# A two-block transformer kernel on one Trainium2 core: the first pair's products moved into the last gz block, attention's reciprocal and scaling moved ahead of the delta rule's side work, the sink column copied by ScalarE

## The reference, cut to what matters

```python
proj = h @ w_in[l]                      # -> gq, gk, gv, gz, ga, gb, sq, sk, sv
o_g = gated_delta_rule_chunked(q_g, k_g, v_g, g, beta)    # 8 heads of 64, chunks of 64
o_g = rms_norm(o_g, gdn_norm_w[l]) * silu(heads(gz))
# inside the delta rule, per head and chunk:
A  = where(strict, einsum('cd,sd->cs', kb, k) * decay, 0)
qk = where(causal, einsum('cd,sd->cs', q, k) * decay, 0)
# sliding window attention, window 128, 8 query heads on 2 key heads:
s = einsum(q, k) * D ** -0.5 - slopes * dist              # alibi and mask
m = maximum(max(s), sink)
p = exp(s - m);  p = p / (sum(p) + exp(sink - m));  o = p @ v
mixed = concatenate([o_g, o_s]) @ w_out[l]
```

## Time and profile before

| | us |
|---|---|
| median of 3 runs | 1262.69 (1262.55 to 1263.47) |
| the profiled execution | 1261.78 |
| its span | 1259.9 |
| TensorE busy | 1217.9 |
| VectorE busy | 706.5 |
| ScalarE busy | 496.3 |
| POOL busy | 107.1 |

### The profile page before, as it was taken

One profiled execution on the slowest core, in us unless ns is written; L12 is line 12 of the kernel. 1 busy time (PEld: TensorE's weight loads), 2 busy tenths in 40 slices (PEclk: granted clock), 3 DMA queues, 4 the chain that ended last, 5 costly groups with the idle time before them and its releaser, 6 DMA issues.

```text
span 1259.9 us, 20097 instructions
## 1 busy us (share of the span) xinstructions
PE 1217.9 (97%) x8477; PEld 998.4 (79%) x8477; DVE 706.5 (56%) x1031; ACT 496.3 (39%) x780; POOL 107.1 (9%) x151
## 2 busy tenths in 40 slices
PE   3899999999999999999999999999999999999998
PEld 3577788788878888888888889798877678888886
DVE  4699878655467453333323457858566555333344
ACT  4543543565246322212222344223465663232232
POOL 4000003621020000000000110000012310000000
PEclk9899999999999999999999999999999999999999
DMA  9665621002123534233322343333222125333311
GB/s 313 211 222 177 218 79 36 3 3 71 35 67 101 167 102 141 75 117 101 100 88 64 88 144 97 101 84 60 78 68 54 27 64 133 101 88 92 114 38 67
DMA packets 150953, 125.60 MB, mean 100 GB/s; under 512 B 16984, under 2 KB 134513, under 8 KB 150736
## 3 DMA queue, kind: packets, MB, share of 16 engines
q1 hardware_dynamic: 147888, 119.88, 31.6%
q10 hardware_dynamic: 1744, 2.36, 0.5%
q0 software_dynamic: 1232, 2.07, 0.5%
HBM read 122.20 MB, written 2.10 MB: 99 GB/s over the span
## 4 chain that ended last, share of the span: by engine, by line
PE 91%; DVE 3%; ACT 2%; DMA 2%; issue 1%; POOL 0%; ACTq 0%; DVEq 0%; POOLq 0%
PE bank L588 56%; PE bank L681 5%; PE bank L830 5%; PE bank L1293 4%; PE bank L1263 4%; PE bank L1327 3%; PE bank L1182 2%; DMA arena<-in_meta_tokens_dram 1%; PE bank L1014 1%; PE bank L1218 1%; PE bank L1235 1%; PE bank L1195 1%; PE bank L802 1%; PE bank L639 1%; PE bank L789 1%
## 5 line engine op out<-in xcount | busy, mean ns | idle before, releaser
L588 PE MATMUL bank<-hsplit,whi 128*128 128x512 f32 (+1 forms) x1872 | 552.0, 379 | 0.8 <-DVE wlo L2051 0.7
L588 PEld LDWEIGHTS bank<-hsplit,whi 128*128 128x128 f32 x1872 | 341.1, 188 | 73.0 <-issue 8.0
L588 PE MATMUL bank<-hsplit,wlo 128*128 128x512 f32 (+1 forms) x936 | 352.3, 376 | 0.0
L2051 DVE TENSOR_TENSOR wlo<-ring,whi 128x2048 fp32r<-128x2048 f32 (+4 forms) x100 | 200.4, 2005 | 180.0 <-ACT whi L1524 179.7
L1524 ACT ACTIVATE whi<-ring 128x2048 fp32r<-128x2048 f32 (+4 forms) x100 | 168.5, 1685 | 133.2 <-DVE xT L2411 53.3
L588 PEld LDWEIGHTS bank<-hsplit,wlo 128*128 128x128 f32 x936 | 175.9, 188 | 33.1
L588 PE MATMUL bank<-a_split,whi 128*128 128x512 f32 x340 | 104.7, 389 | 0.0
L588 PEld LDWEIGHTS bank<-a_split,whi 128*128 128x128 f32 x340 | 63.8, 188 | 13.2
L588 PE MATMUL bank<-a_split,wlo 128*128 128x512 f32 x170 | 66.1, 389 | 0.0
L2080 DVE SCALAR_TENSOR_TENSOR post<-ring,small,post 128x512 f32<-128x512 f32 x77 | 57.9, 752 | 3.2 <-DMA ring<-in_w_ada_dram 0.5
L1465 POOL TENSOR_TENSOR acc<-acc,tb 128x512 f32<-128x512 f32 x12 | 17.7, 1477 | 424.1 <-ACT tb L1763 424.1
(11 more groups left out here) (456 smaller groups left out, 1731.9 us busy)
## 6 DMA issues: line engine op xcount, KB each, us to landing
ring<-in_w_ada_dram SPq DMA_DIRECT2D x24, 1024.0 KB, 5.4
ring<-in_w_in_dram SPq DMA_DIRECT2D x22, 1024.0 KB, 5.3
ring<-in_w_in_dram SPq DMA_DIRECT2D x34, 512.0 KB, 4.7
ring<-in_w_gate_dram SPq DMA_DIRECT2D x11, 1024.0 KB, 5.3
ring<-in_w_up_dram SPq DMA_DIRECT2D x11, 1024.0 KB, 5.4
ring<-in_w_down_dram SPq DMA_DIRECT2D x8, 768.0 KB, 5.0
ring<-in_w_down_dram SPq DMA_DIRECT2D x8, 640.0 KB, 4.6
ring<-in_w_out_dram SPq DMA_DIRECT2D x4, 1024.0 KB, 5.4
```

What stands on the lines that cost most here:

```text
L588: last = mm(o[0:m, 0:n], w[:, k, c0:c0 + m], rhs(s, k), start=k + i == 0, stop=k == kn - 1 and i == 2)
L2051: split_lo = splitter(dve, None, lambda lo, src, hi: tt(lo, src, hi, ALU.subtract))
```

## The change

`chunk_products(0)` (kk and kq of pair 0) and `chunk_turns(0)` (kt and vt) go into the last gz tile, after its steps 3 and 5; pairs 1 to 3 stay where they were. `gate_rows` of pairs 1, 2 and 3 move one or two steps earlier. VectorE takes the reciprocals of units 0, 1 and 2 before `sides_out(2)`, `sides_out(3)` and the last step instead of inside `window`. POOL's `window(j)` stands before the pair's three products instead of behind them. The copy of the sink column goes from VectorE to ScalarE, between vs and kdup.

```diff
--- before.py
+++ after.py
@@ -751,9 +751,41 @@
                     last = mm(query_tile[:, c:c + 2], hsq[(9 + m) % 2][:, b * P:(b + 1) * P], cst("two"), start=True, stop=True)
                 last.then_inc(*(fill("sqsum") if m == 3 else signal("sqsum_step", m)))
 
+            both_heads = (slice(0, HD), slice(HD, P))
+
+            def product(o, left, right, chunks=range(NC), width=CH, start=True, stop=True):
+
+                for i, n in enumerate(chunks):
+                    for r in both_heads:
+                        last = mm(o[r, i * width:(i + 1) * width], left[r, n, :], right(n)[r], start=start, stop=stop)
+                return last
+
+            def tile_product(name, j, left, right):
+
+                o = open_tile(pe, name, j)
+                product(o, left, lambda n: right[:, n, :]).then_inc(*fill(name, j))
+
+            eye = cst("eye")
+
+            def turned(name, j, left):
+
+                o = open_tile(pe, name, j)
+                product(o, left, lambda n: eye).then_inc(*fill(name, j))
+
+            q_of, k_of, v_of = ([by_chunk(qkv[:, 4 * s + j, :]) for j in range(NJ)] for s in range(3))
+
+            def chunk_products(j):
+                pe.wait_ge(*done("silu", 8 + j))
+                tile_product("kk", j, k_of[j], k_of[j])
+                tile_product("kq", j, k_of[j], q_of[j])
+
+            def chunk_turns(j):
+                turned("kt", j, k_of[j])
+                turned("vt", j, v_of[j])
+
             amid_sq = [{}, {3: [(query_lengths, 0)]}, {3: [(query_lengths, 1)]}, {1: [(query_lengths, 2)], 4: [(ada, 8)]}]
             amid_gz = [{1: [(ada, 9)], 3: [(query_lengths, 3)], 5: [(gate_cols,)], 7: [(gate_rows, 0)]},
-                       {3: [(gate_rows, 1)]}, {1: [(gate_rows, 2)], 7: [(gate_rows, 3)]}, {}]
+                       {1: [(gate_rows, 1)]}, {0: [(gate_rows, 2)], 6: [(gate_rows, 3)]}, {3: [(chunk_products, 0)], 5: [(chunk_turns, 0)]}]
             for m in range(4):
                 project(("sq", m), f"sq{m // 2}", P * (m % 2), P, hx, T, release=m % 2 == 1, between=amid_sq[m])
             for m in range(4):
@@ -821,15 +853,6 @@
                 if 0 <= u - 5 < len(SWU) and SWU[u - 5][1] == 3:
                     let_go("so", SWU[u - 5][0])
 
-            both_heads = (slice(0, HD), slice(HD, P))
-
-            def product(o, left, right, chunks=range(NC), width=CH, start=True, stop=True):
-
-                for i, n in enumerate(chunks):
-                    for r in both_heads:
-                        last = mm(o[r, i * width:(i + 1) * width], left[r, n, :], right(n)[r], start=start, stop=stop)
-                return last
-
             all_quarters = ((0, 0), (1, 1), (0, 1), (1, 0))
 
             def heads_to_chunks(name, j, left, right):
@@ -854,27 +877,11 @@
 
             product_order = [(i, b) for i in range(2) for b in range(NB)]
 
-            def tile_product(name, j, left, right):
-
-                o = open_tile(pe, name, j)
-                product(o, left, lambda n: right[:, n, :]).then_inc(*fill(name, j))
-
-            eye = cst("eye")
-
-            def turned(name, j, left):
-
-                o = open_tile(pe, name, j)
-                product(o, left, lambda n: eye).then_inc(*fill(name, j))
-
-            q_of, k_of, v_of = ([by_chunk(qkv[:, 4 * s + j, :]) for j in range(NJ)] for s in range(3))
-
             for j in range(NJ + 1):
                 if j < NJ:
-                    pe.wait_ge(*done("silu", 8 + j))
-                    tile_product("kk", j, k_of[j], k_of[j])
-                    tile_product("kq", j, k_of[j], q_of[j])
-                    turned("kt", j, k_of[j])
-                    turned("vt", j, v_of[j])
+                    if j:
+                        chunk_products(j)
+                        chunk_turns(j)
                 if j:
                     pe.wait_ge(*copied("kk", j - 1))
                     turned("tA", j - 1, gE[j - 1])
@@ -1424,6 +1431,7 @@
             chunked = lambda name: cst(name).unsqueeze(1).broadcast_to([P, NC, CH])
             times = lambda out, a, b, op=ALU.mult: nc.gpsimd.tensor_tensor(out, a, b, op)
             for j in range(NJ + 1):
+                window(j)
                 if j < NJ:
                     pool.wait_ge(*copied("rows", j, 2))
                     pool.wait_ge(*filled("kq", j))
@@ -1438,7 +1446,6 @@
                         pool.wait_ge(*filled("rows", 3, 2))
                     pool.wait_ge(*done("dT", j))
                     times(inv[j], chunked("eye"), gW[j], ALU.subtract).then_inc(*signal("p0", j))
-                window(j)
             pool.wait_ge(*filled("vs"))
             pool.wait_ge(*filled("ada", 9))
             for j in range(NJ):
@@ -1695,6 +1702,9 @@
                 act.wait_ge(*filled(name, j))
                 A(dst, by_chunk(bank(name, j)[:, :]), ACT.Copy).then_inc(*(passed or read(name, j)))
 
+            act.wait_ge(*arrived("gate", 3))
+            act.wait_ge(*filled("gz", 3))
+            A(sc[:, :, SINK], sinks, ACT.Copy).then_inc(*signal("sinkcol"))
             act.wait_ge(*done("dve_vectors", "skn"))
             for g in range(2):
                 for p in range(2):
@@ -2260,8 +2270,8 @@
             def window(u):
                 if u == 0:
                     dve.wait_ge(*arrived("alibi"))
-                    link(v.tensor_copy(sc[:, :, SINK], sinks))
-                if 0 <= u - 2 < len(SWU):
+                    dve.wait_ge(*done("sinkcol"))
+                if u > NJ and 0 <= u - 2 < len(SWU):
                     sw_sum(u - 2)
                 if u < len(SWU):
                     sw_bias(u)
@@ -2324,6 +2334,8 @@
                     decay_arg(j + 1)
                 decay_mul(j)
             for j in range(NJ + 1):
+                if j >= 2:
+                    sw_sum(j - 2)
                 if j < NJ:
                     sides_out(j)
                 if j:
```

## The result

| | before | after |
|---|---|---|
| median of 21 runs, us | 1262.55 (1261.16 to 1264.40) | 1264.71 (1262.30 to 1266.99) |
| after / before | | 1.0017, 95% interval 1.0011 to 1.0023 |
| the profiled execution, us | 1261.78 | 1264.37 |
| its span, us | 1259.9 | 1262.4 |

The change makes the kernel 2.2 us slower (1.4 to 2.9 by the interval): clear of the noise, but within the 0.2% called "no change". The forecast of 1264.0 us is 0.7 us too low; the range held.

What follows compares the result with a forecast made beforehand. TensorE was taken to bound the kernel, busy 1217.9 of 1259.9 us. A new gap of 3.4 plus clock 1.5, less the old gap 2.1 and its clock 1.5, gave +1.3 us: 1264.0 us, range 1262.3 to 1266.0.

Steps and rivals of the forecast that it cites:

- gap before the first scores: TensorE would wait for ScalarE's key copies before the first scores, near 207 to 210 us: 3.4 us.
- low clock behind it: After the new gap TensorE's clock would run low, costing 1.5 us, bounded between 0 and 3.4.
- old gap: TensorE's 2.1 us wait for POOL's scaling of the second unit, near 226 us, would disappear.
- its clock: The low TensorE clock behind the wait for POOL's scaling, 1.5 us, would disappear with that wait.
- The cover moved away: The first pair's 3.88 us of TensorE work would no longer hide ScalarE's key copies, which end 3.88 us later.
- Rival 1: From 210 us on TensorE's clock stays low longer or falls again: 3.4 us lost, 1265.9 us; chance 0.17.
- Rival 3: The wait for the key copies comes but the clock holds: 1262.9 us; chance 0.09.
- Moved in front of the block's last steps they cost PE the same: The first pair's products and turns, 3.88 us, would take TensorE no longer inside the last gz block.
- So the gap goes in any case, mostly because PE is late itself: Even without gain from reordering, the second unit's scaled tile, at 229.2, would precede TensorE, at 229.4 us.
- VectorE "2.75 us later" and "PE 4.9": VectorE's windows start 2.75 us later, TensorE runs 4.9 us late, so waits for PSUM banks don't bind.
- The sink column on ScalarE: ScalarE's new sink copy, ahead of the key copies, would delay them by 0.1 us, at most 0.21.
- Rival 2: POOL stretches small VectorE operations and a scaled tile comes late: TensorE loses 0.2 to 0.7 us, 1264.6 us; chance 0.08.

Runs made afterwards that it cites:

- e2: Changed kernel without the reordering and with the sink copy back on VectorE, leaving the move and the gate rows; 1265.69 us, ratio 1.0022 to the kernel before.
- e8: Changed kernel with only the first pair's products in the gz block, its turns kept behind vs; 1260.32 us, ratio 0.9981 to the kernel before.
- e3b: Changed kernel with five filler matmuls ahead of TensorE's wait for the key copies; 1263.44 us, ratio 1.0002 to the kernel before.
- e1: Changed kernel with the first pair's products and turns put back behind the last gz block; 1258.41 us, ratio 0.9965 to the kernel before.
- e5: Kernel before with only the reordering and the earlier gate rows, sink copy left on VectorE; 1259.73 us, ratio 0.9975.
- e9: Kernel before with nothing but the gate rows one or two steps earlier; 1262.05 us, ratio 0.9996.
- e4: Changed kernel with the first pair's products and turns at one place of the gz block instead of two; 1264.53 us, ratio 1.0014 to the kernel before.
- e3: Changed kernel with seven filler matmuls ahead of TensorE's wait for the key copies; 1263.36 us, ratio 1.0003 to the kernel before.
- e7: Changed kernel with the second pair's products and turns ahead of the first scores on TensorE; 1262.09 us, ratio 0.9994 to the kernel before.
- e6: Kernel before with only the sink copy on ScalarE and the earlier gate rows, old order; 1262.16 us, ratio 0.9998.

## Why the prediction was right or wrong

The forecast was right in direction, range and mechanism; one term of its sum was put at nothing and measured 0.60 us. The stretch adds up by the prediction's own terms:

| term | forecast | measured in after | shown by itself by |
|---|---|---|---|
| gap before the first scores | 3.4 | 3.30 | e2 (3.20), e8 (1.29) |
| low clock behind it | 1.5 (0 to 3.4) | 1.52 | e3b (0), e2 (2.63) |
| old gap | -2.1 | -2.10 | e1, e5, e9 |
| its clock | -1.5 | -1.48 | e1, e5 |
| gz block interrupted twice | 0 | +0.60 | e4 |
| sum | +1.3 | +1.84 (stretch: +1.83) | |

The median moved by 2.2 us, 0.3 more than the stretch; its interval (1.4 to 2.9) holds both, so nothing further is shown. Each gap costs some 0.07 us more from start to start than its wait; in the sum the new one and the old one cancel.

*The cover moved away*: right in place, cause and size. ScalarE's queue was followed correctly, and e1 shows it from the other side: with pair 0 behind the block, the keys' copies cost TensorE nothing.

*The low clock*: 1.52 against 1.5. This precision is luck in part: the same kind of gap (3.20 us) cost 2.63 us in e2, where the low clock lasted 6.8 us, as long as around the first projection, the row that gave the upper bound. So the middle value was fair and the spread real. Rival 1 (from 2.7 us of clock loss on) was close to what e2's profile shows, though it is not what happened in after. Rival 3, gap without clock loss, did not happen behind any gap of 2 us or more; at this place only the fillers of e3 and e3b held the clock.

*"Moved in front of the block's last steps they cost PE the same"*: **this step failed.** TensorE took 11.39 us from L729 to vs; without the move it is 6.92 (e9, 195.64 to 202.56) and 3.87 for the pair, 10.79 in all. The 0.60 us lie at the seams. The projection step behind each group takes 0.81 us instead of 0.69 (202.75 to 203.56), the piece ahead of each is longer too (200.42 to 200.74 is 0.32 instead of 0.23), and each group of 64 lasts 2.01 (200.74 to 202.75, 204.34 to 206.35) instead of 1.92 and 1.96. No wait is recorded there, so what TensorE does at the seams stays open. It is most of what was missing: forecast +1.3, measured +1.83 in the stretch, less the 0.1 us by which the gap was forecast too long.

*"So the gap goes in any case, mostly because PE is late itself"*: mostly, but not in any case. By e2, where only lateness acts, 1.63 of the 2.10 us go and 0.47 remain. The forecast had the tile at 229.2 and TensorE at 229.4 there, a margin too thin to lean on. It took the tile's lateness as fixed at VectorE's 2.75 us, but VectorE waits for TensorE: in e2 the tile came 4.9 us late (231.18 + 0.61, less 196.01, against 225.88 + 0.61, less 195.57), with VectorE's first window 3.4 us late (213.04 - 196.01, against 209.20 - 195.57). In after the gap went altogether because the reordering has the tile ready early, by 3.2 us even where TensorE is not late (e1; e5 without ScalarE's copy: 3.15). I had called the reordering a part that the sum does not need; in truth it is the only part that wins anything by itself, 3.66 us. Had I priced it alone, the better kernel would have stood in the prediction.

*VectorE "2.75 us later" and "PE 4.9"*: VectorE's first window started at 213.42, 3.33 us later than before (209.20 + 0.89). The difference to 2.75 is the 0.60 us of the interrupted block. Its third pair's side work starts 4.6 us later (221.51 against 216.03 + 0.89): it waits for TensorE, whose clock was low, and so has little lateness of its own. The idle time before alibi is 6.00 us, as forecast. Alibi, due at 211.9, came at 212.5 (213.42 less 0.89), again the 0.60. The bank waits that the prediction excluded did not come in after, and did come in e7.

*The sink column on ScalarE*: its price (0.1) was right. Without the move the gain for VectorE is real for 5 us and gone after that (e6); on the time it is nothing. With the move there is hardly a gain: in e2 POOL was idle and the copy took 0.18 us on VectorE, as the prediction's paragraph on small operations had said of such a case. In after this part of the change is a loss of 0.1 us. Rival 2's stretched negations did happen in e6 (1.09 us) and in after (0.99 us at 234.08), without TensorE waiting for them, since in after the margins behind the reordering are 1.7 us or more (third unit: scaled at 231.86 + 0.61 = 232.47, turned at 234.22).

*The gate rows*: nothing, as forecast (e9).

## What to carry to other kernels

Moving work to before the end of a block delays all that waits for the end, and also removes that work as cover behind it; ask of each engine what it does between the block's end and the first consumer, and if the two sides of a change can be split, forecast each alone. A gap can cost its length plus the clock behind it, so with half the move (e8, a gap of 1.29 us without clock loss) the change won 1.9 us where with the whole it lost 1.8; without any move it won 3.7. An engine freed for a microsecond gives that on only if its next waits are not set by the engine that it feeds.

## What the runs showed of the hardware that was not expected

- Where the clock fell: not behind gaps of 1.29 us (e8) and 1.01 us (e7), but behind 2.07 to 2.11 us (before, e6, e9; about 1.5 us lost) and 3.20 to 3.30 us (after, e4: 1.52; e2: 2.63). The spread at nearly equal gaps was over 1 us. It goes with how long the clock was low: some 3.4 us in after, e4, before, e6 and e9, 6.8 us in e2. No run here says why it fell early there.
- A VectorE copy of 128x8 took 1.10 and 1.12 us beside a POOL product (before, e5) and 0.18 us with POOL idle (e2).
- A group of 64x64 matmuls put between 128x512 ones cost 0.31 us (e8) for one and 0.60 us for two interruptions, with no wait recorded.
- Around the first projection (49 us) the clock is low at different times from execution to execution of equal work: from 46.1 to 52.9 us in before, from 48.0 to 54.8 in after. That and what else precedes the change moved the stretch's start from 195.6 to 197.6 us over the profiled executions (e9 195.64, e5 197.64). A single span can't judge an edit of 1 us; a stretch between two fixed instructions can.
